# Differential heads gathered with the queries on the partitions and normed there, with rotary halves turned by DMA and narrow weights split inside one tile

## The chip, the cores and the metric

The kernel runs on one core of one Trainium2 chip. The metric is the device time of one launch, in microseconds (us); lower is better. The program is the same for every input, and all its arithmetic is done in one launch. The engines are written as the profile writes them: PE is TensorE (PEld its weight loads), DVE is VectorE, ACT is ScalarE, POOL is GpSimd, SP is the queue that issues nearly all transfers.

## The reference, cut to what matters

Three blocks run one after the other on 512 tokens of width 1024, in float32. The first has gated linear attention, a depthwise convolution of 31 taps and a spatial gate beside each other, then a feed-forward part. The second has two layers, each of feed-forward, a mixer and feed-forward. The third has a recurrent unit and blockwise attention. The change touches the two mixers most:

```
def _apply_rope(t, cos, sin):
    t1, t2 = jnp.split(t32, 2, axis=-1)
    rot = jnp.concatenate([-t2, t1], axis=-1)
    return (t32 * cos + rot * sin).astype(t.dtype)

def _hybrid_mixer(h, w_in, forget_bias, ..., subln, w_out, lambda_init):
    proj = h @ w_in
    fq, fk, fv, ff, dq, dk, dv = jnp.split(proj, IN_OFFSETS, axis=-1)
    log_f = jax.nn.log_sigmoid((ff + forget_bias).astype(jnp.float32))   # ff: 8 columns
    cum_f = jnp.cumsum(log_f.transpose(0, 2, 1), axis=-1)
    q_d = _apply_rope(to_heads_d(dq), cos, sin)
    k_d = _apply_rope(to_heads_d(dk), cos, sin)
    ...
    o_f, o_d = _causal_block_attention(q_f, k_f, v_f, cum_f, q_d, k_d, v_d, lam)
    o_d = _rmsnorm(o_d, subln) * (1.0 - lambda_init)      # over the 128 values of a head
    return jnp.concatenate([o_f, o_d], axis=-1) @ w_out

def layer_norm(x, g, b):                                  # after the convolution, over 1024 channels
    xc = xf - jnp.mean(xf, axis=-1, keepdims=True)
    ...
def gla_log_gates(a_dn, a_up, a_b):                       # a_dn: 2 x 16 columns
    z = jnp.einsum('bler,erk->blek', a_dn.reshape(bsz, L, 2, GLA_RANK), a_up) + a_b
```

There are four differential heads (two queries and two keys of 64, values of 128) and eight forgetting heads of 64 in each mixer.

## The kernel before

**Layout.** Activations lie with their channels on the partitions, so that a tile is 128 channels by 512 tokens. Products with weights keep float32's precision by splitting: every activation tile is held as a rounded part and a rest (`A.hi`, `A.lo`), every weight tile too (`WH`, `WL`), and three matmuls replace one (`products`, lines 1180 to 1182, and `K`, lines 1199 to 1201, where the tokens come out on the partitions). All other matmuls are plain float32.

**The weight pipeline.** A unit is a weight tile of 128 by 1024. SP loads it into one of five `raw` buffers, ACT rounds it into one of three `WH` (line 1574), POOL writes the rest into `WL` (line 2658), and PE uses both. ACT and POOL work two units ahead of PE in the program, SP up to seven. ACT can round a unit only when PE has used the one three before.

**The order of work.** One function, `program`, is run once for each engine; each engine's class implements the steps that it takes part in. So every engine has a fixed order, and an instruction that waits holds all behind it on its engine. Semaphores are set from events by name.

**The mixer (`second`).** With the units numbered from its start: `ff` (the forget gate; its 8 columns are padded to 128) and `dqk 0` together, the means for the norm (`roots`, line 1236), `dqk 4`, the row of norm factors (`row`, line 1266), then `diff_in` of both, `forget`, and four `K` units of `dv`, the values. `forget` is a chain of small operations on DVE and ACT that ends in running sums (`CUM`), which 16 transfers copy to the forgetting heads' queries and keys. Then come the other `dqk` tiles and `fv`. `rope(L, n)` turns tile `n` of `DQ`: PE multiplies by a constant matrix `rot` (line 1476), DVE multiplies the result by the sines, POOL multiplies the tile by the cosines in place and adds.

**Attention (`attend`).** A job is a head and a block of 128 queries: `scores` (PE, line 1486, then the mask, line 1489), a softmax over DVE and ACT, `turn` (PE transposes, line 1499, ACT copies), `gather` (PE, line 1513). Jobs are staggered: a block is turned two or three steps after its scores, and gathered later still. In each step a generator gives PE half a unit of projections (12 matmuls) to do beside, and one step of `diff_norm`. For a differential head the gather holds the values and streams the turned weights:

```
m = e.matmul(bo[a:z, qt * 128:qt * 128 + 128], at.value(h, kt, c), at.T.of(name)[:, kt * 128:kt * 128 + 128], start=kt == 0, stop=kt == qt)
```

so its output has the head's 128 values on the partitions. ACT copies it to `OD`; `diff_norm` then squares it (ACT), sums over the partitions by four matmuls against the constant `mean` (PE, line 1236), takes the root (ACT) and the reciprocal (DVE), spreads the factors over all partitions by four matmuls (PE, line 1266), copies that row (ACT) and multiplies twice (DVE).

**The convolution's norm.** PE forms the mean over all channels in one bank by eight matmuls, one for each tile of `CA` (line 1459).

## Time and profile before

| | |
|---|---|
| median of 3 runs | 3498.76 us (3498.42 to 3500.62) |
| profiled execution, its own time | 3496.82 us |
| span from its first to its last instruction | 3494.8 us |
| PE busy | 3428.0 us, 98% of the span |
| POOL busy | 1465.1 us, 42% |
| ACT busy | 1252.4 us, 36% |
| DVE busy | 1230.5 us, 35% |
| granted TensorE clock, mean of the span | 0.991 of full speed |
| read from HBM | 336.02 MB, 97 GB/s |

The table is read by shares: one engine is busy nearly all the time, the other three under half of it. A matmul is pipelined, so what it costs PE is read from the start of one to the start of the next, not from its duration. A float32 matmul that is not split shows as two records.

### The profile page before, as it was taken

What the parts mean: (1) busy time and instruction counts of PE and PEld (TensorE: products, weight loads), DVE (VectorE), ACT (ScalarE), POOL (GpSimd) and SP (SyncE); (2) the same over time, 40 slices, a digit from 0 to 9 for tenths busy, and PEclk for the clock granted to TensorE, in tenths of its full rate; (3) what the DMA queues carried; (4) which work ended last, traced back from release to release, by engine and by line L of the source; (5) the groups of instructions that cost most, each with busy time, mean ns of one, the idle gap of its engine ahead of it and who ended that gap; (6) DMA issues with size and microseconds to landing.
All of it is one profiled execution on the core that took longest, in us unless ns stands there. A gap on an engine that the chain in (4) does not pass through costs nothing.

```text
span 3494.8 us, 38815 instructions
## 1 busy us (share of the span) xinstructions
PE 3428.0 (98%) x15932; PEld 2744.4 (79%) x15932; DVE 1230.5 (35%) x2137; ACT 1252.4 (36%) x1942; POOL 1465.1 (42%) x668
## 2 busy tenths in 40 slices
PE   8999999999999999999999999999999999999998
PEld 5767787887888887887777888888887778888776
DVE  3266764523221144212653111211114652111644
ACT  4534323523222332223454222322233543222544
POOL 4323444554444444445323444444435224444332
PEclk9999999999999999999999999999999999999999
DMA  7211233442333323333113333333332023333211
GB/s 273 64 55 61 97 97 127 144 145 73 129 127 123 97 96 140 130 98 103 52 34 103 97 95 94 96 98 97 93 96 94 28 76 97 97 94 100 73 61 55
DMA packets 99291, 341.15 MB, mean 98 GB/s; under 512 B 11371, under 2 KB 11755, under 8 KB 98956
## 3 DMA queue, kind: packets, MB, share of 16 engines
q1 hardware_dynamic: 98352, 336.97, 29.8%
q8 instruction: 126, 2.06, 0.2%
q10 hardware_dynamic: 764, 1.72, 0.1%
q14 instruction: 49, 0.40, 0.0%
HBM read 336.02 MB, written 2.10 MB: 97 GB/s over the span
## 4 chain that ended last, share of the span: by engine, by line
PE 92%; DVE 2%; ACT 2%; DMA 1%; issue 1%; POOL 1%; SPq 0%; ACTq 0%; DVEq 0%
PE ps L1180 26%; PE ps L1182 25%; PE ps L1181 25%; PE ps L1199 2%; PE ps L1201 2%; PE ps L1200 2%; PE ps L1486 2%; PE ps L1513 1%; PE ps L1499 1%; DMA t<-in_w_f1i 1%; POOL t L2658 1%; PE ps L1397 0%; PE ps L1266 0%; PE ps L1411 0%; DMA t<-in_w_ada 0%
## 5 line engine op out<-in xcount | busy, mean ns | idle before, releaser
L2658 POOL TENSOR_TENSOR t<-t,t 128x1024 fp32r<-128x1024 f32 (+2 forms) x588 | 1360.9, 2316 | 1932.3 <-ACT t L1574 1931.0
L1180 PE MATMUL ps<-t,t 128*128 128x512 f32 (+1 forms) x4048 | 1608.9, 397 | 17.7 <-POOL t L2658 8.0
L1182 PE MATMUL ps<-t,t 128*128 128x512 f32 (+1 forms) x4048 | 1584.5, 391 | 0.0
L1181 PE MATMUL ps<-t,t 128*128 128x512 f32 (+1 forms) x4048 | 1578.9, 390 | 0.0
L1180 PEld LDWEIGHTS ps<-t,t 128*128 128x128 f32 x4048 | 763.7, 189 | 196.5 <-issue 27.7
L1182 PEld LDWEIGHTS ps<-t,t 128*128 128x128 f32 x4048 | 762.8, 188 | 167.9
L1181 PEld LDWEIGHTS ps<-t,t 128*128 128x128 f32 x4048 | 764.2, 189 | 158.0 <-issue 1.4
L1574 ACT CAST t<-t 128x1024 fp32r<-128x1024 f32 (+2 forms) x588 | 584.2, 995 | 576.1 <-PE ps L1182 414.8
L2451 DVE TENSOR_TENSOR t<-t,ps 128x512 f32<-128x512 f32 x110 | 75.7, 688 | 528.8 <-PE ps L1182 513.7
L1643 ACT CAST t<-t 128x512 fp32r<-128x512 f32 x158 | 97.0, 621 | 393.2 <-DVE t L2451 355.7
L1834 ACT ACTIVATE t<-t 128x512 f32<-128x512 f32 x88 | 55.6, 632 | 316.8 <-DVE t L2444 316.7
L2042 DVE TENSOR_TENSOR t<-t,t 128x512 fp32r<-128x512 f32 x138 | 119.6, 871 | 119.9 <-ACT t L1643 119.9
L2280 DVE SCALAR_TENSOR_TENSOR ps<-t,t,ps 128x392 f32<-128x392 f32 (+14 forms) x232 | 159.0, 686 | 6.2
L2412 DVE TENSOR_TENSOR t<-ps,t 128x512 f32<-128x512 f32 x32 | 22.1, 692 | 381.5 <-PE ps L1182 381.5
L2444 DVE TENSOR_TENSOR t<-ps,t 128x512 f32<-128x512 f32 x88 | 60.7, 690 | 251.0 <-PE ps L1182 225.1
L1199 PE MATMUL ps<-t,t 128*128 128x512 f32 x336 | 136.9, 407 | 8.6 <-DVE t L2188 3.9
L1871 ACT ACTIVATE t<-ps,t 128x128 f32<-128x128 f32 (+3 forms) x160 | 86.4, 544 | 151.9 <-PE ps L1499 66.3
L1201 PE MATMUL ps<-t,t 128*128 128x512 f32 x336 | 132.6, 395 | 0.0
L1200 PE MATMUL ps<-t,t 128*128 128x512 f32 x336 | 132.6, 395 | 0.0
L2507 DVE TENSOR_REDUCE t<-ps 128x1 f32<-128x128 f32 (+3 forms) x160 | 77.6, 485 | 73.3 <-PE ps L1489 72.2
L1816 ACT ACTIVATE t<-t,t 128x512 fp32r<-128x512 f32 x48 | 34.8, 724 | 157.2 <-DVE t L2414 107.5
L2094 DVE SCALAR_TENSOR_TENSOR t<-t,t,t 128x1024 f32<-128x1024 f32 x49 | 74.2, 1514 | 31.2 <-DMA t<-in_w_ada 31.1
(291 smaller groups left out, 2220.6 us busy)
## 6 DMA issues: line engine op xcount, KB each, us to landing
t<-in_w_f1i SPq DMA_DIRECT2D x88, 512.0 KB, 3.8
t<-in_w_f2i SPq DMA_DIRECT2D x88, 512.0 KB, 3.7
t<-in_w_ada SPq DMA_DIRECT2D x72, 512.0 KB, 4.6
t<-in_w_ffi SPq DMA_DIRECT2D x44, 512.0 KB, 3.9
t<-in_w_f1o SPq DMA_DIRECT2D x32, 512.0 KB, 3.5
t<-in_w_f2o SPq DMA_DIRECT2D x32, 512.0 KB, 3.5
t<-in_w_gate SPq DMA_DIRECT2D x24, 512.0 KB, 4.4
t<-in_w_out SPq DMA_DIRECT2D x48, 256.0 KB, 2.7
```

The lines of the kernel that those rows point to most:

```text
L1180: e.matmul(out, wh[:, at], X.hi[c][:, 0:N], start=c == first, stop=False)
L1181: e.matmul(out, wh[:, at], X.lo[c][:, 0:N], start=False, stop=False)
L1182: m = e.matmul(out, wl[:, at], X.hi[c][:, 0:N], start=False, stop=c == final)
L1199: e.matmul(out, X.hi[c][:, at], wh[:, w], start=c == 0, stop=False)
L1200: e.matmul(out, X.hi[c][:, at], wl[:, w], start=False, stop=False)
L1201: m = e.matmul(out, X.lo[c][:, at], wh[:, w], start=False, stop=c == 7)
L1574: e.copy(k.WH[:, n % NHL, 0:w], k.raw[:, j % NRAW, 0:w]).then_inc(*k.rounded.inc(('rounded', j)))
L1643: e.copy(A.hi[t], src).then_inc(*k.act.inc(('hi', A.tag, t)))
L1871: e.activation(p[:, 0:n], self.bank('s', *key)[:, 0:n], ACT.Exp, scale=at.root(h, qt, c) if h[0] == 'm' else 0.125, bias=st[:, 1:2], accum ...
L2042: e.tensor_tensor(A.lo[t], src, f(A.hi[t]), ALU.subtract).then_inc(*k.dve.inc(('lo', A.tag, t), *events))
L2280: e.scalar_tensor_tensor((c3 if j == 30 else a3)[:, :, lo:hi], h3[:, :, lo + w - 15:hi + w - 15], param(k, 'conv_w', w * 8 + i), a3[:, :, ...
L2658: e.tensor_tensor(k.WL[:, n % NHL, 0:w], k.raw[:, j % NRAW, 0:w], f(k.WH[:, n % NHL, 0:w]), ALU.subtract).then_inc(*k.rest.inc(('rest', j) ...
```

## The change

It has six parts.

1. **Rotary by DMA.** The matmul with `rot` goes. SP copies the two halves of each group of 64 partitions crosswise into a buffer by four transfers of 32 partitions; the sign is in the table of sines. DVE multiplies that buffer by the sines in place; two buffers take turns. There are 8 tiles in each of 2 layers.
2. **Narrow weights.** For `a`, `ff0` and `ff1` the rest of the weights (at most 32 columns) is written beside the rounded part in the same `WH` tile, so a unit needs two matmuls for each of its 8 blocks in place of three (`thin`). The two partial results come out on other partitions: for `a` the next matmul adds them (its contraction grows from 33 to 65 rows), for `ff` DVE does, with two more operations in `forget`.
3. **The mean of the convolution.** POOL adds the eight tiles into `R[0]` by seven additions, spread over the `sv` units; one matmul follows.
4. **Gather and norm of the differential heads.** The gather holds the turned weights and streams the values, so the queries lie on the partitions. ACT copies the bank to a buffer, squares it in four pieces with a sum over each row, and takes the root; DVE inverts and scales; PE transposes four blocks; ACT copies them to `OD` with the gain as a scale.
5. **Running sums.** Two transfers with a repeated source replace 16, issued behind the units of `fv` in place of before those of `dv`.
6. **Waits.** The copy of a differential head's output and the mean's copy on DVE no longer wait for the running sums and for a buffer.

```diff
+    sign = np.where(i % 64 < 32, -1.0, 1.0).astype(np.float32)[:, None]
+    cs = np.stack([np.cos(emb), sign * np.sin(emb)], axis=1).astype(np.float32)
...
+THIN = ('a', 'ff0', 'ff1')
...
+                    if n or kp:
+                        on.conv_sum(4 * n + kp)
...
+    on.cum_loads(L)
...
+            for j in range(3):
...
-    def forget(self, L, R, last):
+    def cum_loads(self, L):
         k, e = (self.k, self.e)
         self.wait_ge('forgot', L)
-        for h in range(8):
-            e.dma_start(k.QF[72:80, h, :], k.CUM[0:8, 0, :]).then_inc(*load(k, 'cum').inc(by=16))
-            e.dma_start(k.KF[64:72, h, :], k.CUM[0:8, 1, :]).then_inc(*load(k, 'cum').inc(*([('load', 'cum', L)] if h == 7 else []), by=16))
+        q, kk = (k.CUM[0:8, i:i + 1, :].broadcast_to([8, 8, S]) for i in range(2))
+        e.dma_start(k.QF[72:80, :, :], q).then_inc(*load(k, 'cum').inc(by=16))
+        e.dma_start(k.KF[64:72, :, :], kk).then_inc(*load(k, 'cum').inc(('load', 'cum', L), by=16))
+    def rope(self, L, n):
+        k, e = (self.k, self.e)
+        m = self.take(rope_ring(k, L), 'turn', L, n)
+        self.wait_ge('diff in', L, n)
+        turned = load(k, f'turned {n}')
+        for p in (0, 64):
+            e.dma_start(m[p:p + 32, :], k.DQ[p + 32:p + 64, n, :]).then_inc(*turned.inc(by=16))
+            e.dma_start(m[p + 32:p + 64, :], k.DQ[p:p + 32, n, :]).then_inc(*turned.inc(*([('turned half', L, n)] if p else []), by=16))
...
+    def thin(self, out, i, h, X, ks, c0, N, first, final):
+        k, e = (self.k, self.e)
+        wh = k.WH[:, h % NHL]
+        self.wait_ge('rest', i)
+        for c in ks:
+            at = slice(128 * (c - c0), 128 * (c - c0) + 128)
+            self.wait_ge('lo', X.tag, c)
+            e.matmul(out, wh[:, at], X.hi[c][:, 0:N], start=c == first, stop=False)
+            m = e.matmul(out, wh[:, at], X.lo[c][:, 0:N], start=False, stop=c == final)
...
-            for j in range(KT):
-                self.wait_ge('tap', j, 30)
-                m = e.matmul(b, const(k, 'mean'), k.CA[:, j, :], start=j == 0, stop=j == KT - 1)
-            m.then_inc(*k.filled.inc(('filled', ('mu',))))
+            self.wait_ge('conv sum', KT - 1)
+            e.matmul(b, const(k, 'mean'), k.R[0], start=True, stop=True).then_inc(*k.filled.inc(('filled', ('mu',))))
...
-    def rope(self, L, n):
-        k, e = (self.k, self.e)
-        b = self.take(k.banks, 'rot', L, n)
-        self.wait_ge('diff in', L, n)
-        e.matmul(b, const(k, 'rot'), k.DQ[:, n, :], start=True, stop=True).then_inc(*k.filled.inc(('filled', ('rot', L, n))))
...
-                m = e.matmul(bo[a:z, qt * 128:qt * 128 + 128], at.value(h, kt, c), at.T.of(name)[:, kt * 128:kt * 128 + 128], start=kt == 0, stop=kt == qt)
+                turned, values = (at.T.of(name)[:, kt * 128:kt * 128 + 128], at.value(h, kt, c))
+                held, moved = (turned, values) if h[0] == 'd' else (values, turned)
+                m = e.matmul(bo[a:z, qt * 128:qt * 128 + 128], held, moved, start=kt == 0, stop=kt == qt)
...
-        sq = diff_sum(at, i)
-        if j == 1:
-            self.roots(sq, 2, 8.0)
+        k, e, tag = (self.k, self.e, ('hn', at.tag, i))
         if j == 2:
-            self.row(sq)
+            b, m = (self.take(k.banks, 'turned out', at.tag, i), at.N.of(tag))
+            self.wait_ge('od scaled', at.tag, i)
+            for t in range(4):
+                x = e.transpose(b[:, t * 128:t * 128 + 128], m[:, t * 128:t * 128 + 128], const(k, 'ident'))
+            x.then_inc(*k.filled.inc(('filled', ('turned out', at.tag, i)), ('free', tag)))
...
+            m = self.take(at.N, 'hn', at.tag, i)
             self.wait_ge('filled', key)
-            self.wait_ge('load', 'cum', at.tag)
-            e.copy(k.OD[:, i, :], self.bank(*key)).then_inc(*k.act.inc(('od', at.tag, i), ('free', key)))
+            e.copy(m, self.bank(*key)).then_inc(*k.act.inc(('od', at.tag, i), ('free', key)))
...
-            m = self.take(at.N, 'hn', at.tag, i)
+            c = self.take(k.cols, 'cols', tag)[:, 0:4]
             self.wait_ge('od', at.tag, i)
-            e.activation(m, k.OD[:, i, :], ACT.Square).then_inc(*k.act.inc(('ssq', ('hn', at.tag, i), 0)))
-        if j == 1:
-            self.roots(diff_sum(at, i), 2, 8.0)
+            self.wait_ge('load', 'cum', at.tag)
+            for t in range(4):
+                w = slice(t * 128, t * 128 + 128)
+                e.activation(k.OD[:, i, w], at.N.of(tag)[:, w], ACT.Square, accum_out=c[:, t:t + 1]).then_inc(*k.act.inc())
+            self.settle()
+            e.activation(c, c, ACT.Sqrt, scale=1.0 / 128, bias=unit(k, 2)).then_inc(*k.act.inc(('root', tag)))
         if j == 2:
-            self.row(diff_sum(at, i))
+            self.wait_ge('filled', ('turned out', at.tag, i))
+            self.wait_ge('load', 'cum', at.tag)
+            e.activation(k.OD[:, i, :], self.bank('turned out', at.tag, i), ACT.Copy, scale=k.sm[:, 69:70]).then_inc(*k.act.inc(('diff normed', at.tag, i), ('free', ('turned out', at.tag, i))))
...
-    return ring(k, 'turn ' + L, k.tmp[2:3], [('forgot', L)])
+    return ring(k, 'turn ' + L, [k.R[2], k.SQ], [('filled', ('d', 'f1_' + L, 7))])
...
-        e.tensor_tensor(x, self.bank('ff', L)[0:8, :], R.acc[0:8, :], ALU.mult).then_inc(*k.dve.inc(('forget scaled', L), ('free', ('ff', L))))
+        e.tensor_tensor(x, self.bank('ff', L)[0:8, :], R.acc[0:8, :], ALU.mult).then_inc(*k.dve.inc())
+        e.tensor_tensor(y, self.bank('ff', L)[32:40, :], R.acc[32:40, :], ALU.mult).then_inc(*k.dve.inc(('free', ('ff', L))))
+        self.settle()
+        e.tensor_tensor(x, x, y, ALU.add).then_inc(*k.dve.inc(('forget scaled', L)))
...
-        m = self.take(rope_ring(k, L), 'turn', L, n)
+        m = rope_ring(k, L).of(('turn', L, n))
         self.wait_ge('load', 'cs', L)
-        self.wait_ge('filled', ('rot', L, n))
-        e.tensor_tensor(m, self.bank('rot', L, n), k.CS[:, 1, :], ALU.mult).then_inc(*k.dve.inc(('rope sine', L, n), ('free', ('rot', L, n))))
+        self.wait_ge('turned half', L, n)
+        e.tensor_tensor(m, m, k.CS[:, 1, :], ALU.mult).then_inc(*k.dve.inc(('rope sine', L, n)))
...
-        if j == 3:
-            self.wait_ge('row', tag)
-            e.scalar_tensor_tensor(x, x, param(k, 'subln_' + at.tag), diff_sum(at, i).acc, ALU.mult, ALU.mult).then_inc(*k.dve.inc(('free', tag)))
+            c = k.cols.of(('cols', tag))[:, 0:4]
+            self.wait_ge('root', tag)
+            e.reciprocal(c, c).then_inc(*k.dve.inc())
             self.settle()
-            e.tensor_scalar(x, x, at.scale, None, ALU.mult).then_inc(*k.dve.inc(('diff normed', at.tag, i)))
+            e.tensor_tensor(halves(at.N.of(tag)), halves(at.N.of(tag)), c.rearrange('p (a n) -> p a n', n=1).broadcast_to([128, 4, 128]), ALU.mult).then_inc(*k.dve.inc(('od scaled', at.tag, i), ('free', ('cols', tag))))
...
+                if src[1] in THIN:
+                    raw, wh = (ap.rearrange('p (c m) -> p c m', m=128) for ap in (k.raw[:, j % NRAW, :], k.WH[:, n % NHL, :]))
+                    e.tensor_tensor(wh[:, :, 32:64], raw[:, :, 0:32], f(wh)[:, :, 0:32], ALU.subtract).then_inc(*k.rest.inc(('rest', j), ('read', j)))
+                    continue
...
+    def conv_sum(self, i):
+        k, e = (self.k, self.e)
+        if i == 1:
+            self.wait_ge('normed', 'cx', 7)
+            self.wait_ge('tap', 0, 30)
+        else:
+            self.wait_ge('conv sum', i - 1)
+        self.wait_ge('tap', i, 30)
+        e.tensor_tensor(k.R[0], k.CA[:, 0, :] if i == 1 else k.R[0], k.CA[:, i, :], ALU.add).then_inc(*k.pool.inc(('conv sum', i)))
...
```

Three places show how instructions moved. The first is DVE in the mixer of layer 0, from the scaling of the first two tiles of `DQ` (`diff_in`, t_120) through `forget` to the first sines (t_129). Before:

```order
L2484 TENSOR_TENSOR t_120<-ps,t_71 128x512 [waits s_filled,s_act]
L2484 TENSOR_TENSOR t_120<-ps,t_71 128x512 [waits s_filled]
L2468 MEMSET t_130 8x512
L2471 TENSOR_TENSOR t_62<-ps,t_71 8x512
L2473 SCALAR_TENSOR_TENSOR t_63<-t_62,t_64 8x512 [waits s_act]
L2475 SCALAR_TENSOR_TENSOR t_65<-t_130,t_63 8x512 [waits s_dve]
L2477 TENSOR_SCALAR t_131<-t_65 8x512 [waits s_dve]
L2478 TENSOR_SCALAR t_131<-t_65 8x512
L2491 TENSOR_TENSOR t_64<-ps,t_129 128x512 [waits s_filled,s_load16,s_dve]
```

The same place in the changed kernel (its line numbers are its own):

```order
L2505 TENSOR_TENSOR t_120<-ps,t_71 128x512 [waits s_filled,s_act]
L2505 TENSOR_TENSOR t_120<-ps,t_71 128x512 [waits s_filled]
L2486 MEMSET t_130 8x512
L2489 TENSOR_TENSOR t_62<-ps,t_71 8x512
L2490 TENSOR_TENSOR t_63<-ps,t_71 8x512
L2492 TENSOR_TENSOR t_62<-t_62,t_63 8x512 [waits s_dve]
L2494 SCALAR_TENSOR_TENSOR t_63<-t_62,t_64 8x512 [waits s_act]
L2496 SCALAR_TENSOR_TENSOR t_65<-t_130,t_63 8x512 [waits s_dve]
L2498 TENSOR_SCALAR t_131<-t_65 8x512 [waits s_dve]
L2499 TENSOR_SCALAR t_131<-t_65 8x512
L2512 TENSOR_TENSOR t_72<-t_72,t_129 128x512 [waits s_load19,s_load16]
```

Two operations stand between the first scaling and the point at which ACT may start its part of `forget` (the wait for s_act), and the sine waits for transfers in place of PE. The second place is SP's queue in the same stretch. Before, behind the loads of `dqk`:

```order
L1053 DMA t_53<-in_w_dv 128x1024
L1053 DMA t_53<-in_w_dqk 128x1024 x2
L1104 DMA t_117<-t_131 8x512
L1105 DMA t_118<-t_131 8x512
L1104 DMA t_117<-t_131 8x512
```

And in the changed kernel (t_72 and t_93 are the two buffers of the turned halves):

```order
L1052 DMA t_53<-in_w_dv 128x1024
L1052 DMA t_53<-in_w_dqk 128x1024 x2
L1052 DMA t_53<-in_w_fv 128x1024 x2
L1113 DMA t_72<-t_120 32x512
L1114 DMA t_72<-t_120 32x512
L1113 DMA t_72<-t_120 32x512
L1114 DMA t_72<-t_120 32x512
L1052 DMA t_53<-in_w_fv 128x1024
L1113 DMA t_93<-t_120 32x512
```

The 16 small transfers ahead of `fv` are gone, and groups of four stand between the loads of weights. The third place is PE in attention, at the second matmul group of the first differential head's norm. Before (a group like it, L1236 x4, stands one step ahead):

```order
L1182 MATMUL ps<-t_50,t_55 128x512
L1266 MATMUL ps<-t_56,t_69 128x128 x4
L1486 MATMUL ps<-t_120 128x512 x2
L1489 MATMUL ps<-t_61 128x128 x2
L1513 MATMUL ps<-t_62,t_121 128x128 x3
L1499 MATMUL ps<-t_56,t_127 128x128
```

And in the changed kernel, where nothing stands one step ahead:

```order
L1191 MATMUL ps<-t_50,t_55 128x512
L1539 MATMUL ps<-t_56,t_65 128x128 x4
L1499 MATMUL ps<-t_120 128x512 x2
L1502 MATMUL ps<-t_61 128x128 x2
L1528 MATMUL ps<-t_121,t_62 128x128 x3
L1512 MATMUL ps<-t_56,t_127 128x128
```

Four transposes stand where the four matmuls of the row stood, and the gather (L1513, now L1528) has its two operands exchanged.

## Rows read from the trace of the kernel before

**Rows 1.** The page: PE's busy time, and the chain by engine.

```profile
PE 3428.0 (98%) x15932; PEld 2744.4 (79%) x15932; DVE 1230.5 (35%) x2137; ACT 1252.4 (36%) x1942; POOL 1465.1 (42%) x668
PE 92%; DVE 2%; ACT 2%; DMA 1%; issue 1%; POOL 1%; SPq 0%; ACTq 0%; DVEq 0%
```

**Rows 2.** Timeline of PE, products in a feed-forward part, first and last of 15.

```profile
999.71 0.39 PE L1180 MATMUL ps<-t,t 128*128 128x512 f32 x1
...
1002.88 0.39 PE L1182 MATMUL ps<-t,t 128*128 128x512 f32 x1
```

**Rows 3.** Timeline of PE, products of unit `a` for the context.

```profile
52.99 0.28 PE L1180 MATMUL ps<-t,t 128*128 128x256 f32 x1
53.11 0.28 PE L1181 MATMUL ps<-t,t 128*128 128x256 f32 x1
```

**Rows 4.** Timeline of PE, around `rot` in the value units and in attention.

```profile
1625.60 1.02 PE L1476 MATMUL ps<-t,t 128*128 128x512 f32 x2
...
1626.69 0.40 PE L1200 MATMUL ps<-t,t 128*128 128x512 f32 x1
...
1678.91 1.02 PE L1476 MATMUL ps<-t,t 128*128 128x512 f32 x2
1679.86 1.13 PE L1486 MATMUL ps<-t 64*128 64x512 f32 x4
```

**Rows 5.** Timeline of PE, the convolution's mean.

```profile
559.63 7.03 PE L1459 MATMUL ps<-t,t 128*128 128x512 f32 x16
```

**Rows 6.** Timeline of POOL, a weight rest before that mean.

```profile
553.81 2.41 POOL L2658 TENSOR_TENSOR t<-t,t 128x1024 fp32r<-128x1024 f32 x1 [3.09 <-ACT t L1574]
```

**Rows 7.** Timeline of PE, a head's norm, and four transposes.

```profile
1694.20 0.60 PE L1499 MATMUL ps<-t,t 128*128 128x128 f32 x4
...
1712.74 0.95 PE L1236 MATMUL ps<-t,t 128*128 128x2 f32 x8
1713.62 0.92 PE L1486 MATMUL ps<-t 64*128 64x384 f32 x4
...
1718.26 1.05 PE L1266 MATMUL ps<-t,t 128*128 128x128 f32 x8
1719.25 1.13 PE L1486 MATMUL ps<-t 64*128 64x512 f32 x4
```

**Rows 8.** The chain in order of time, 1588 to 1660 us.

```profile
1609.89 0.55 DVE t L2471
...
1615.84 0.95 ACT t L1574
1616.86 3.12 POOL t L2658
```

**Rows 9.** Timeline of PE, the same stretch.

```profile
1618.17 1.02 PE L1476 MATMUL ps<-t,t 128*128 128x512 f32 x2
...
1620.03 0.50 PE L1199 MATMUL ps<-t,t 128*128 128x512 f32 x1 [0.83 <-POOL t L2658]
```

**Rows 10.** Timeline of PE, two waits elsewhere.

```profile
265.67 0.50 PE L1199 MATMUL ps<-t,t 128*128 128x512 f32 x1 [3.90 <-DVE t L2188]
802.94 0.79 PE L1180 MATMUL ps<-t,t 128*128 128x512 f32 x1 [3.20 <-DVE t L2042]
```

**Rows 11.** Windows: length, busy time of each engine (records), granted clock, DMA.

```profile
89.00:95.00 6.00, 6.00 (x13) 4.13 (x13) 0.00 (x0) 5.13 (x8) 0.00 (x0) 0.50 0.01 3
262.00:272.00 10.00, 6.33 (x21) 5.08 (x22) 6.86 (x11) 6.68 (x9) 4.26 (x2) 0.83 0.09 20
798.00:812.00 14.00, 10.80 (x36) 8.32 (x35) 1.45 (x2) 3.13 (x4) 8.25 (x4) 0.76 0.35 110
1660.00:1780.00 120.00, 120.00 (x648) 91.75 (x647) 71.48 (x211) 59.00 (x142) 40.83 (x22) 1.00 0.14 45
```

**Rows 12.** Line 1104: the queue's time for one transfer of running sums.

```profile
L1104 SPq DMA_DIRECT2D t<-t x16: 624/624/729, 1622.8 to 2636.0; - x16
```

**Rows 13.** Transfers: issues, KB each, median us to landing.

```profile
out<-t SPq DMA_DIRECT2D x8, 256.0 KB, 2.0
```

More of the change, by code:

```diff
@@ L54, in shape_constants @@
     c['causal'] = np.where(t <= s, 0.0, NEG)
-    rot = np.zeros((128, 128))
-    for b in (0, 64):
-        for j in range(32):
-            rot[b + 32 + j, b + j] = -1.0
-            rot[b + j, b + 32 + j] = 1.0
-    c['rot'] = rot
     c['hmean'] = same / 64.0
@@ L812, in norms @@
                 yield
-            for j in range(4):
+            for j in range(3):
                 on.diff_norm(at, j, i)
@@ L2706, in rope @@
         self.wait_ge('load', 'cs', L)
-        self.wait_ge('filled', ('rot', L, n))
+        self.wait_ge('turned half', L, n)
         e.tensor_tensor(x, x, k.CS[:, 0, :], ALU.mult).then_inc(*k.pool.inc())
```

43 lines of the change are left out of this document (20 added, 23 removed).

## The prediction

> **What bounds the kernel now.** I read the page first. PE is busy for 98% of the span and the chain that ended last runs 92% over PE [rows 1]. So an instruction taken from PE is worth its time unless PE then waits for another engine, and an instruction added elsewhere costs nothing unless PE comes to wait for it. The second view is PE's timeline, for prices: a matmul is worth the time from its start to the next start. Fourteen steps between products take 3.17 us [rows 2], 0.226 us each; with 256 columns it is 0.12 [rows 3]. The third view is the chain in the mixer, to find where PE is not the one that sets the pace. It shows one such place: from `forget` the chain goes over DVE and ACT, ACT's rounding of a weight tile, POOL's rest of it, and only then to PE [rows 8], which sat idle 0.83 us [rows 9]. The fourth is the granted clock, because long waits of PE were followed by half clock [rows 10, 11].
>
> **Narrow weights.** Each of the four units loses 8 of 24 matmuls. `a` for the context has 256 columns: 8 × 0.12 = 0.9 us. `a` for the tokens, `ff0` and `ff1`: 24 × 0.226 = 5.4. Sum 6.4 us. POOL's part of such a unit shrinks too. I take the whole.
>
> **Rotary.** One `rot` matmul in the value units moves the product after the next from 1625.60 + 0.226 to 1626.69: 0.86 us. In attention it is 0.95 to the next group [rows 4]. There are 16: four in the value units and four in attention of each layer. The first of each layer is worth nothing, for it lies in front of the wait above: PE could have begun the next unit at 1618.2, where `rot` stands, but the weights were there only at 1620.0 [rows 9]. So each layer gains 3 × 0.86 + 4 × 0.95 = 6.4 us, together 12.8. If that wait did not exist it would be 14.5.
>
> In place of the matmul, SP issues four transfers. Its own row for a small copy inside SBUF is 0.62 us of queue [rows 12], so 2.5 us for a tile. Their landing is not in the trace; the nearest row below is the store of 256 KB, 2.0 us [rows 13], and I take that, so a tile is turned about 4.5 us after SP reaches it. At the upper end I allow twice that, 4 us of landing, if a load of weights goes ahead of it. Who waits: POOL, which stands before its cosines with the next weights behind them. In layer 0 SP may issue the first group only when the rest of the third unit of `dv` is written: 1616.86 + 3.12 [rows 8], and 1.3 later by the term on `forget` below, so 1621.3. Turned at 1626, cosines and sum done at 1629 (two passes of 128 by 512, half a weight rest each), the weights behind them (2.4 us [rows 6]) at 1631; PE wants them two units of 24 products after it began at 1621.3, so at 1632. So the cover is about 1 us for the first tile and more for the others, and I cost it at nothing. In attention DVE waits for the transfers with a softmax behind it; it waits there for the matmul already, PE turns a block two or three steps after its scores, and a step is 5.5 us (1712.74 to 1718.26 [rows 7]), which covers a delay of 2 to 3 us.
>
> **The mean.** Sixteen records take 7.03 us [rows 5]; two remain, so 14/16, 6.0 us with the drain left out. POOL takes on seven additions of 128 by 512, half the size of its weight rests of 2.4 us, so 1.2 to 1.5 us each. It idles about 3 us before each of those rests [rows 6], and the last `sv` unit leaves it time before the mean. Nothing is added.
>
> **The head's norm.** Sums cost PE 1713.62 − 1712.74 = 0.88 us, the row 1719.25 − 1718.26 = 0.99. Four transposes take 0.60 us with the drain and one alone 0.27, so 0.35 to 0.4 [rows 7]. Net 1.47 for a head, 11.7 us for eight. The gather keeps its count and shape, 128 by 128 by 128, with operands exchanged: nothing. ACT takes four squares with sums in place of one, about 0.8 us more, and has the root's table load in the same step; DVE has one pass in place of two. The scaled block is asked for one step later, and I take no wait. The lower end of this term is nothing gained, if each head's transposes wait 1.5 us.
>
> **`forget`.** Here the change costs. Two more DVE operations, each about as long as L2471 (0.55 to 0.62 us [rows 8]) and one settled on the other, put 1.3 us in front of ACT's chain, and ACT's rounding of the next weights stands behind that. So PE begins the third `dv` unit 1.3 us later than before, counted from the row of norm factors. Two layers: +2.6 us. The fewer transfers of running sums are worth nothing: the loads of `fv` behind them came in time.
>
> **The clock.** The wait of PE at that place grows. It was 0.83 us after a `rot` of 1.02; without `rot` and with 1.3 us more it is 0.83 + 0.86 + 1.3 = 3.0 us. The waits of 3.90 and 3.20 us [rows 10] lie in stretches where the clock was 0.83 over 10 us and 0.76 over 14 [rows 11], that is 1.7 and 3.4 us lost at 1.2 in place of 2.4 GHz. A wait of 3.0 us is near the short end of those that lost it, so I take it to happen in one of the two layers at 2.5 us, and keep none (0) and both at 3.4 us (6.8) for the range.
>
> **Sum.** −6.4 − 12.8 − 6.0 − 11.7 + 2.6 + 2.5 = −31.8 us. The profiled execution took 3496.8 us with a span of 3494.8; it lies 1.9 us under the median of the runs. Its sum is 3465.0; against the median, 3498.8 − 31.8 = 3467.0 us, which I predict.
>
> **Rivals.**
>
> (a) *Turned halves come late.* If the landing is 4 us or more, POOL's next weights miss PE by 1 to 2 us at the first two tiles of each layer, 4 to 8 us in all, and one wait may take the clock with it. For it: the cover is 1 us by my own count, and SP may send a load of weights just before. Against: 64 KB are little. It gives 3471 to 3480, say 3475. Chance 0.19.
>
> (b) *The clock is kept where it was lost.* After the 33-row matmuls for `a` the window 89 to 95 us ran at half clock with PE never idle [rows 11]. The change puts matmuls of 65 rows in place of those before that window; whether the clock then holds, no row shows. Those 6 us would pass in 3, so it is worth 3 us at most; with no loss in the mixers either it is 3467 − 2.5 − 3 = 3461.5. Chance 0.12.
>
> (c) *The head's norm gains nothing*, because the transposes wait for ACT's longer block and DVE's scaling. ACT is busy 59 of 120 us in that stretch and DVE 71 [rows 11], which speaks against it. 3467 + 11.7 = 3479. Chance 0.06.
>
> (d) *Transposes take the clock down.* In 1660 to 1780 us PE ran many transposes and the granted clock was 1.00 throughout [rows 11], so four more in a block should not matter. Price if each of eight heads lost the 2.5 us above: +20 us, 3487. Chance 0.02. The Trainium skill (TensorE: Matmul & The Clock Gate, Part 4: PE-mode transpose) says that a transpose does not bring the engine to its full clock as other matmuls do. By that rule the sum is 3487, by the row 3467; the trace so far goes against the rule for transposes mixed with products.
>
> (e) *Slower than before: the queue in attention.* DVE stands before each turned half with softmax work behind it. If the transfer comes later than the two steps (11 us) by which PE runs ahead, PE idles, some 3 us, and loses the clock for 2.5. With four tiles in attention of each layer that is 8 × 5.5 = 44 us, so 3511. It decides from a landing of about 8 us on (11 less 2.5 of issue); the store in rows lands in 2. Chance 0.02.
>
> **How the numbers follow.** My forecast, with no, one or two losses of clock, covers 3464 to 3471 and has 0.59. (a) 0.19, (b) 0.12, (c) 0.06, (d) and (e) 0.02 each. The range reaches down to (b), less 2 us for the lower end of what `forget` costs, and up to the middle of (a) and near (c): 3459 to 3478 leaves out about 0.15. About 0.2% (7 us) is what a measurement of this kernel can tell from no change. Everything but (e) is faster by more than that, and I keep a little for what I have not seen: faster 0.95, same 0.03, slower 0.02.
>
> **What would show each step.** PE records: 14 fewer at the mean, none at L1476's place, 32 fewer products, four one-record transposes for each head at 0.35 to 0.4 us. PE's wait before the third `dv` unit of each layer near 3 us, released by POOL, and the clock behind it. POOL's wait before its first cosines, to see whether the turned halves come about 4.5 us after SP reaches them. No new wait of PE for DVE or ACT before the transposes. I would be wrong if small copies inside SBUF cost SP or land much later than the rows nearest to them, or if PE's waits in attention grow.

## The result, and the profile after

The changed kernel took 3480.65 us (median of four runs, 3473.08 to 3481.17) beside 3498.59 of the kernel before: ratio 0.9946, 95% interval 0.9934 to 0.9958. It is faster by 17.9 us, where 31.8 were forecast, and 2.65 us above the upper end of the range. Measured again later, beside other runs of the kernel before, the same program took 3467.8 us (3466.04 to 3473.29, ratio 0.9923, interval 0.9911 to 0.9936). The second time lies 0.8 us from the forecast of 3467.0, but, as the last sections show, with other terms than the forecast's. So there are two things to explain: terms of the sum that are not there in any profile, and one that is there in some executions and not in others.

The page of the changed kernel, its line of PE and the chain by engine, answers to [rows 1]:

```profile
PE 3391.5 (98%) x15758; PEld 2721.9 (78%) x15758; DVE 1255.3 (36%) x2135; ACT 1257.6 (36%) x1998; POOL 1472.4 (42%) x675
PE 87%; DVE 4%; ACT 2%; DMA 2%; issue 1%; POOL 1%; SPq 0%; DVEq 0%; ACTq 0%; POOLq 0%
```

PE lost 36.5 us of work and the span (3478.5 us) only 16.3. PE's share of the chain fell from 92% to 87%: what went is not idle time spread thin, it is a few places where another engine now ends last. PE's waits, in us in total, times, longest:

```profile
PE ps L1189 <- POOL t L2682: 17.0, 9, 4.3
...
PE ps L1189 <- ACT t L1883: 4.8, 4, 1.6
PE ps L1220 <- DVE t L2206: 4.3, 1, 4.3
```

The timeline of PE has them one by one. These are the largest of those that are new or longer than before (the second answers to the first of [rows 10], the fourth to [rows 9]; the two near 1700 and 1711 us come again in layer 1):

```profile
101.63 0.51 PE L1189 MATMUL ps<-t,t 128*128 128x512 f32 x1 [2.37 <-POOL t L2682]
264.59 0.80 PE L1220 MATMUL ps<-t,t 128*128 128x512 f32 x1 [4.31 <-DVE t L2206]
622.35 0.80 PE L1189 MATMUL ps<-t,t 128*128 128x512 f32 x1 [3.69 <-POOL t L2682]
1617.79 0.50 PE L1220 MATMUL ps<-t,t 128*128 128x512 f32 x1 [3.05 <-POOL t L2682]
1700.22 0.50 PE L1189 MATMUL ps<-t,t 128*128 128x512 f32 x1 [0.83 <-ACT t L1883]
1711.04 0.50 PE L1189 MATMUL ps<-t,t 128*128 128x512 f32 x1 [1.57 <-ACT t L1883]
2613.25 0.50 PE L1220 MATMUL ps<-t,t 128*128 128x512 f32 x1 [3.05 <-POOL t L2682]
3241.81 0.80 PE L1189 MATMUL ps<-t,t 128*128 128x512 f32 x1 [4.26 <-POOL t L2682]
```

To see what each place costs I cut the spans at landmarks that PE has in every kernel (the first K unit behind the gates, the norm rows, the lambda matmul) and subtracted their start times. Length in us, and in brackets what of it was lost at half clock:

| stretch | before | before again | changed | changed again |
|---|---|---|---|---|
| start to the K unit at 264 | 265.7 (10.2) | 266.6 (13.7) | 264.6 (7.3) | 264.9 (9.3) |
| to the row at 663 (the mean is in it) | 398.4 (1.7) | 396.7 (0) | 398.6 (4.6) | 393.7 (2.7) |
| from there to layer 0's norm row | 942.3 (6.8) | 938.4 (5.1) | 939.5 (5.1) | 936.1 (5.1) |
| norm row to lambda, layer 0 / 1 | 37.6 / 37.6 | 37.6 / 37.7 | 39.7 (1.7) / 39.1 | 39.7 / 39.7 (1.7) |
| lambda to the row behind attention, layer 0 / 1 | 246.6 / 246.6 | 246.6 / 246.6 | 238.1 / 238.1 | 239.7 (1.7) / 238.1 |
| from there to layer 1's norm row | 719.5 | 719.5 | 717.7 | 717.7 |
| row behind layer 1's attention to the end | 600.5 (11.9) | 600.5 (11.9) | 603.1 (13.7) | 601.8 (13.7) |

Attention comes out alike to 0.1 us once the clock is taken off. The changed kernel's mixers do not (38.0 to 39.7 us), nor does the mean's stretch: 5 us lie between two executions of one program. The profiled execution of the repeat took 3473.29 us, the slowest of its five, so the table does not show what made the median 3467.8.

### The profile page after: what moved, and what is told of

Read it like the earlier page. It is cut to its first block, busy times and chain, and to the rows that moved or that the text cites. A ratio compares the mean times of both kernels' runs of the same rounds, so it can differ in the third digit from the quotient of the medians.

```text
span 3478.5 us, 38566 instructions
## 1 busy us (share of the span) xinstructions
PE 3391.5 (98%) x15758; PEld 2721.9 (78%) x15758; DVE 1255.3 (36%) x2135; ACT 1257.6 (36%) x1998; POOL 1472.4 (42%) x675
## 4 chain that ended last, share of the span: by engine, by line
PE 87%; DVE 4%; ACT 2%; DMA 2%; issue 1%; POOL 1%; SPq 0%; DVEq 0%; ACTq 0%; POOLq 0%
PE ps L1189 25%; PE ps L1191 24%; PE ps L1190 24%; PE ps L1220 2%; PE ps L1221 2%; PE ps L1222 2%; PE ps L1499 2%; PE ps L1528 1%; DVE t L2112 1%; PE ps L1512 1%; POOL t L2682 1%; DMA t<-in_w_ada 1%; DMA t<-in_w_f1i 1%; DMA t<-t 1%; PE ps L1418 1%
## 5 line engine op out<-in xcount | busy, mean ns | idle before, releaser
L1189 PE MATMUL ps<-t,t 128*128 128x512 f32 x4016 | 1598.1, 398 | 31.7 <-POOL t L2682 17.0
L1191 PE MATMUL ps<-t,t 128*128 128x512 f32 x4016 | 1573.0, 392 | 0.0
L1190 PE MATMUL ps<-t,t 128*128 128x512 f32 x4016 | 1568.4, 391 | 0.0
L1220 PE MATMUL ps<-t,t 128*128 128x512 f32 x336 | 136.0, 405 | 14.7 <-POOL t L2682 6.7
L1221 PE MATMUL ps<-t,t 128*128 128x512 f32 x336 | 133.5, 397 | 0.0
L1222 PE MATMUL ps<-t,t 128*128 128x512 f32 x336 | 133.2, 397 | 0.0
L2528 DVE TENSOR_REDUCE t<-ps 128x1 f32<-128x128 f32 (+3 forms) x160 | 77.5, 484 | 67.0 <-PE ps L1502 66.0
L2112 DVE SCALAR_TENSOR_TENSOR t<-t,t,t 128x1024 f32<-128x1024 f32 x49 | 89.2, 1821 | 33.1 <-DMA t<-in_w_ada 33.0
```

The lines of the kernel that those rows point to most:

```text
L1189: e.matmul(out, wh[:, at], X.hi[c][:, 0:N], start=c == first, stop=False)
L1190: e.matmul(out, wh[:, at], X.lo[c][:, 0:N], start=False, stop=False)
L1191: m = e.matmul(out, wl[:, at], X.hi[c][:, 0:N], start=False, stop=c == final)
L1220: e.matmul(out, X.hi[c][:, at], wh[:, w], start=c == 0, stop=False)
L1221: e.matmul(out, X.hi[c][:, at], wl[:, w], start=False, stop=False)
L1222: m = e.matmul(out, X.lo[c][:, at], wh[:, w], start=False, stop=c == 7)
```

## The experiments

The control, the changed kernel unchanged. 

> The changed kernel once more, unchanged. Expected 3480.65 us within 0.1%. Its second profile tells which waits of PE and which falls of the clock belong to the program and which to chance: the theory that the gain is lost in four fixed places expects PE to wait again 3.7 us before the first osgu gate unit (622 us), 2.4 us behind the gate logs of the context (101 us), 3.05 us before the third dv unit of each layer, and 0.8 and 1.6 us in the attention of each layer. The rival, that it is lost by chance falls of the clock, expects these waits to change from run to run.

3467.8 us. The waits at 101 us, before the third `dv` units and in attention came again to 0.1 us. Others did not: at 619.10 PE waited 0.31 us where it had been 3.69, in the last stretch 2.16 where it had been 4.26, and three waits on POOL between 1313 and 1338 us (2.5 us together) were gone, while in layer 0's mixer a wait of 1.39 us was new. So both views were partly wrong: the first places are fixed, the others differ between executions of one program. The chain in order of time shows how it comes about, first in the slower profile:

```profile
597.29 3.64 DMA t<-in_w_ada
...
600.96 3.48 DVE t L2112
...
604.45 3.92 DMA t<-in_w_ada
...
618.73 1.26 POOL t L2688
620.00 2.31 POOL t L2682
...
622.35 0.80 PE ps L1189
```

Beside the `su` units DVE takes one piece of the modulation's sum (L2112) for each unit; the pieces come through one buffer, which SP refills only when DVE has read it. That is a loop: 3.9 us of transfer, then the piece. PE passes a unit in 6.36 us, so the loop keeps up while a piece takes under 2.4. The timelines of POOL and DVE, in the slower profile:

```profile
600.95 2.40 POOL L2682 TENSOR_TENSOR t<-t,t 128x1024 fp32r<-128x1024 f32 x1
600.96 3.46 DVE L2112 SCALAR_TENSOR_TENSOR t<-t,t,t 128x1024 f32<-128x1024 f32 x1 [1.40 <-DMA t<-in_w_ada]
```

and in the faster one:

```profile
600.61 3.38 POOL L2682 TENSOR_TENSOR t<-t,t 128x1024 fp32r<-128x1024 f32 x1
600.40 1.34 DVE L2112 SCALAR_TENSOR_TENSOR t<-t,t,t 128x1024 f32<-128x1024 f32 x1 [1.17 <-DMA t<-in_w_ada]
```

Whoever starts first runs at its own pace, and the other is held: DVE needs 3.46 us in place of 1.34 when it starts 0.01 us behind POOL's weight rest, POOL 3.38 in place of 2.40 when DVE starts first. The Trainium skill (SBUF — State Buffer, section "SBUF: two separate sides") says that GpSimd and a VectorE instruction with two SBUF inputs take one port pair as an exclusive lock for a whole instruction. By that rule the trace agrees to 0.3 us: POOL's 2.40 and then DVE's 1.34 make 3.74 where DVE took 3.46, and POOL, held until DVE ended at 601.74, would take 3.53 where it took 3.38. In all eight profiles with this loop as it stands the same meeting near 600 us tells the two kinds apart: DVE starts 0.01 to 0.05 us behind POOL in the three with the long wait and ahead of it in the other five. Here 0.2 us of a transfer's landing (3.64 against 3.42 us) decided which of the two came first, and with it 5 us of the program: 3.4 of wait and 1.7 of clock.

The mean undone:

```diff
-                    if n or kp:
-                        on.conv_sum(4 * n + kp)
...
-            e.matmul(b, const(k, 'mean'), k.R[0], start=True, stop=True)
+            for j in range(KT):
+                m = e.matmul(b, const(k, 'mean'), k.CA[:, j, :], start=j == 0, stop=j == KT - 1)
```

> The changed kernel with the mean back on TensorE (16 matmuls; no additions on POOL). Theory A: of the 6.0 us that the mean gives PE, 5.2 are given back at the end of the stage, since the weights for the first gate unit behind it come no earlier; so the time rises by 0.8 us only, to about 3481.5, and PE's wait of 3.69 us there is gone. Rival B: the mean is worth its 6.0 us and the missing time is elsewhere: 3486.7 us.

3478.66 us, 10.9 more than the control beside it. The stretch took 399.3 us (2.7 lost at half clock) against 393.7 (2.7): 5.6 us, near B. Against the profile with the long wait (398.6) it is 0.7, as theory A has it, so A holds only where that wait comes. The two profiles as a whole are 5.1 us apart (3476.6 and 3471.5); that the medians are 5.8 more apart has no place that these profiles show.

Half of the sum's pieces put off:

```diff
             conv_norm()
-            ada()
+            if i % 2 == 0:
+                ada()
...
-    branch(on, 1, 'oconv', XA, k.CN, lambda j: ada() if j < 5 else None, done=mixture)
+    branch(on, 1, 'oconv', XA, k.CN, lambda j: ada() if j < 7 else None, done=mixture)
```

> The changed kernel; of the eight pieces of the modulation's sum that VectorE takes beside the eight su units (each reads one side buffer that SyncE may refill only then), four are put off to the oconv branch. Theory A: the loop over that one buffer (VectorE's piece of 2.6 to 3.5 us and 3.9 us from issue to landing, 6.8 us for a turn where PE needs 6.36 for a unit) is what makes VectorE late, and so the rest of the weights at 622 us. Then PE's wait of 3.69 us shrinks to under 1 and the time falls by 4 to 5 us, to about 3476. Rival B: POOL is late because it has the seven additions: the wait stays near 3.7 us and the time at 3480.6.

3471.19 us (3464.12 to 3474.11), no faster than the control: since the control did not have the long wait either, the runs decide nothing. In its profile the wait is gone altogether, the stretch 392.2 us.

The probe of the loop:

```diff
     def side(self, g, kt, since):
         self.wait_ge(*since)
+        if g == 2 and kt > 2:
+            self.wait_ge('mixed', kt - 3)
```

> The changed kernel; SyncE issues each further load of the side buffer of the modulation's sum only behind VectorE's product for the spatial unit two back, 1.5 to 2.5 us later than it could. A probe of the loop over that one buffer. Theory A: the loop is what makes VectorE late, its turn grows from 6.8 us to 8 or more over six turns, and PE waits at 622 us by 5 us or more in all, in every run. Rival B (POOL's seven additions): PE's wait there is what it was in the two profiles, 0.3 or 3.7 us.

3481.2 us. PE waited here too:

```profile
624.18 0.80 PE L1191 MATMUL ps<-t,t 128*128 128x512 f32 x1 [4.41 <-POOL t L2684]
```

Theory A had the wait in every run; one of the six took only 3472.76, and whether it waited is not known. In the profile the wait came, but the size was wrong: the turn grew to 6.85 us only (issues at 579.40, 586.23, 593.09, 599.93, 606.78), because the pieces, pushed to another moment, met less of POOL's rests and took 1.3 to 2.0 us. A loop of 6.85 us gives the wait without any long piece. It is the loop's turn against PE's 6.36 us that matters, and the meeting with POOL is one way to lengthen it. POOL's seven additions are the same where the wait comes and where it does not, so they do not tell the two apart; that they have no share in it is not shown. Of the eight profiles with the additions, all eight pieces and no hold (this one apart), three had the long wait.

The halves' arithmetic (DVE's sine, POOL's cosine and sum) one step behind their transfers, which `turned_half` issues:

```diff
             on.T_part(('dqk', L, n), 'dqk' + L, n, A, 0, 2)
             if turn is not None:
-                on.rope(L, turn)
+                on.turned_half(L, turn)
             yield
             on.T_part(('dqk', L, n), 'dqk' + L, n, A, 1, 2)
+            if turn is not None:
+                on.rope(L, turn)
```

> The changed kernel; in attention the four transfers of a turned half stand where they stood, but VectorE's sine and POOL's cosine and sum stand one step (half a unit) later, so the engines no longer stop in front of the transfer. Theory A: VectorE's wait of 1.6 to 1.7 us for each transfer, with its sine of 1.6 to 2.5 us beside POOL's weight rest, makes the softmax late, and with it the PSUM bank that PE's next product needs: the waits of PE of 0.83 and 1.57 us in each layer go, the time falls by about 5 us to 3476. Rival B: they come from ScalarE's longer block for the head's norm with its two table loads: the 1.57 us stay, the time falls by at most 1.7 us.

3463.17 us. Attention took 234.8 us in both layers in place of 238.1, and both waits were gone. That is 3.2 to 3.3 us for 2.40 of waiting. PE's instructions are the same and in the same order, and compared start by start the wait of 0.83 cost 1.09 us and that of 1.57 cost 1.87 (0.25 more goes ahead of them), so PE loses some 0.3 us beyond the idle time that the profile shows. So A, with a reserve for the second wait that `norm_by_sums` shows below. The timeline of DVE, the changed kernel:

```profile
1696.00 2.50 DVE L2512 TENSOR_TENSOR t<-t,t 128x512 f32<-128x512 f32 x1 [1.60 <-DMA t<-t]
1698.43 0.68 DVE L2528 TENSOR_REDUCE t<-ps 128x1 f32<-128x512 f32 x1
1699.14 0.15 DVE L2534 TENSOR_SCALAR t<-t 128x1 f32<-128x1 f32 x1
```

and POOL beside it, then ACT behind it:

```profile
1695.56 2.39 POOL L2682 TENSOR_TENSOR t<-t,t 128x1024 fp32r<-128x1024 f32 x1 [4.52 <-ACT t L1586]
...
1699.39 0.69 ACT L1883 ACTIVATE t<-ps,t 128x512 f32<-128x512 f32 x1 [3.90 <-PE ps L1512]
```

With the edit the same instruction is

```profile
1690.24 0.69 DVE L2518 TENSOR_TENSOR t<-t,t 128x512 f32<-128x512 f32 x1
```

DVE stood 1.60 us in front of the transfer and was then held by POOL's rest, 2.50 us in place of 0.69. The row maximum (L2528, L2534) came 3.4 us late, ACT's exponential behind it frees the PSUM bank that PE's next product writes, and PE waited 0.83 us at 1700.22. (The row of ACT names PE's transposes, which end at 1699.39 by the same trace; DVE's L2534 ends at 1699.29, and in layer 1 the same row names it.) In the kernel before, where the sine read PSUM, it took 0.69 us at all 16 places, each time with POOL at work beside it, and so it did in `rot_on_pe`:

```profile
1698.51 0.69 DVE L2491 TENSOR_TENSOR t<-ps,t 128x512 f32<-128x512 f32 x1 [2.06 <-PE ps L1476]
```

The rotation back on TensorE, and the head's norm by sums again (each with its own part of the change undone):

```diff
-    e.dma_start(m[p:p + 32, :], k.DQ[p + 32:p + 64, n, :])
...
+    e.matmul(b, const(k, 'rot'), k.DQ[:, n, :], start=True, stop=True)
```

> The changed kernel with the rotation by a matmul again, no transfers of turned halves. Theory A: a rot costs PE 0.82 to 0.9 us, but in attention the waits of 0.83 and 1.57 us that the transfers cause go with them: 3 x 0.82 in the value units and 4 x 0.88 - 2.4 in attention of each layer, 3.6 a layer, so the time rises by 7.2 us; the wait before the third dv unit falls from 3.05 to 2.2 us. Rival B: the transfers gave their full 12.8 us, and the time rises by that.

3474.18 us. Attention took 240.1 us, 2.0 more a layer, its two waits gone; the mixers 39.0 and, with 1.7 at half clock, 40.6, which is 0 to 1 us more for both together. In all 4 to 5 us, so nearer A than B, but under A's 7.2: the waits that A priced at 2.4 us a layer cost 3.2, and in the mixers, where other waits and the clock vary, only part of the second `rot` shows.

```diff
-            for t in range(4):
-                x = e.transpose(b[:, t * 128:t * 128 + 128], m[:, t * 128:t * 128 + 128], const(k, 'ident'))
...
+        if j == 1:
+            self.roots(sq, 2, 8.0)
+        if j == 2:
+            self.row(sq)
```

> The changed kernel with the head's norm and the gather as before (transposed gather, sums of squares and a row by TensorE). By the rows of its own profile a head's norm takes 0.53 us of TensorE (four transposes) where it took 0.88 + 0.98; so PE takes 1.33 us more for a head, 10.6 us for eight. Theory A: the term of the head's norm was about right (11.7 forecast), and the time rises by 9 to 11 us over the changed kernel's 3468 to 3481 us. Rival (c) of the prediction: the new norm gains nothing because its transposes wait; the time does not rise. In between (4 to 7 us): ScalarE's longer block has a share in the waits of 0.83 and 1.57 us of a layer's attention.

3488.76 us. Attention took 243.1 and 243.2 us with the clock taken off: 5.0 a layer, 10.1 in all, theory A. The rest of the time above the control is the long wait at 622 us, which this profile has too, and falls of the clock.

But PE's wait of 1.57 us is gone here as well, though the transfers of rotary are in place; the 0.83 us stayed. The changed kernel's ACT at that place, then ACT and PE's next product in this run:

```profile
1709.13 1.28 ACT L1883 ACT_TABLE_LOAD   x1 [0.84 <-DVE t L2534]
1710.42 0.47 ACT L1883 ACTIVATE t<-ps,t 128x256 f32<-128x256 f32 x1
...
1708.18 0.47 ACT L1884 ACTIVATE t<-ps,t 128x256 f32<-128x256 f32 x1 [3.11 <-DVE t L2528]
1709.27 0.49 PE L1189 MATMUL ps<-t,t 128*128 128x512 f32 x1
```

The new norm's root makes ACT load its table again before the next exponential, 1.28 us between DVE's late maximum and the exponential that PE waits for, and without the sums PE itself comes there 0.8 us earlier. So the second wait needs both parts of the change, the late transfer and the new norm, and goes when either is undone. Undone one at a time the two give 2.0 and 5.0 us a layer, while attention before (246.6) and after (238.1) lie 8.5 apart. Each difference is smaller by the shared wait, so their sum takes it off twice: 1.5 us a layer, 3.0 in all, are missing from it.

The two sides of `forget`:

```diff
-THIN = ('a', 'ff0', 'ff1')
+THIN = ('a',)
...
-        e.tensor_tensor(y, self.bank('ff', L)[32:40, :], R.acc[32:40, :], ALU.mult)...
-        self.settle()
-        e.tensor_tensor(x, x, y, ALU.add)...
```

> The changed kernel with the ff units at full width again (24 matmuls) and without the two added operations of VectorE in the forget chain; a stays narrow. Theory A: the added operations put 1.38 us into the chain that ends at the third dv unit, so that with them gone PE's wait there is 1.7 us in place of 3.05, against 1.8 us more of matmuls: +0.45 us a layer, +0.9 in all, less up to 1.7 for a fall of the clock that does not come. Rival B: the wait there has another cause and stays at 3.05: +3.6 us.

3475.07 us (3463.5 to 3479.1). The wait:

```profile
1616.33 0.50 PE L1220 MATMUL ps<-t,t 128*128 128x512 f32 x1 [1.68 <-POOL t L2679]
```

1.68 where A said 1.7, in the second layer 1.67, and no fall of the clock behind either; the stretch ahead of layer 1 grew by the 1.8 us of matmuls. The mixers took 37.1 and 37.3 us, where the eight profiles with the wait of 3.05 us have 39.6 on average: 2.4 us a layer back for 1.8 of matmuls. So the narrow `ff`, taken with its two operations and the clock behind them, gained nothing and cost about 0.6 us a layer.

```diff
-    on.forget(L, R, last)
     for kp in range(4):
         on.K(('dv', L), 'dv' + L, 0, A, kp, 4)
+        if kp == 0:
+            on.forget(L, R, last)
```

> The changed kernel with the forget chain written behind the first dv unit instead of ahead of it, so that ScalarE rounds the third dv unit's weights before the chain and not after it. Theory A: PE's wait of 3.05 us before the third dv unit goes in both layers, and the fourth unit's weights come in time: 6.1 us faster, and up to 1.7 us more where the clock had fallen behind the wait. Rival B: the wait only moves one unit on (POOL's rests and the turned halves stand behind the same chain): 0 to 2 us faster.

3460.95 us. The mixer's stretch fell to 34.7 us in both layers from 39.1 to 39.7: 9.3 to 10.0 us in all, more than A's 6.1 + 1.7, since a wait of 0.7 or 1.4 us two units further on (1.39 us at 1622 in the control) went too.

The narrow `a` (`THIN = ('ff0', 'ff1')`), and the kernel before again:

> The changed kernel with the two a units at full width again (24 matmuls); ff stays narrow. Theory A: behind each a unit the next weights wait for ScalarE, which has them behind the exponentials and logarithms of the gates, so that PE's wait of 2.37 us at 101 us shrinks by what the matmuls take more; the narrow a units were worth at most the 0.9 us of the context's, and the time to the first K unit behind them (264 us) stays within 1 us. Rival B: they were worth their 2.7 us, and that stretch grows by it.

3473.6 us. PE's wait behind the token's unit:

```profile
102.91 0.50 PE L1189 MATMUL ps<-t,t 128*128 128x512 f32 x1 [0.60 <-POOL t L2682]
```

2.37 − 0.60 = 1.77 us, the eight matmuls (1.81). The windows from the context's gate logs to the next landmark behind that unit, for the kernel before, the repeat of the changed kernel and this run (length, busy time by engine, and the granted clock as the third number from the end):

```profile
85.55:108.85 23.30, 23.30 (x82) 16.95 (x81) 2.53 (x4) 14.19 (x20) 7.15 (x3) 0.85 0.22 71
88.57:109.18 20.61, 18.24 (x73) 13.46 (x72) 2.53 (x4) 14.11 (x20) 7.03 (x3) 1.00 0.21 70
87.83:108.49 20.66, 20.06 (x82) 14.96 (x81) 2.54 (x4) 14.21 (x20) 7.10 (x3) 1.00 0.24 76
```

With wide or narrow `a` the stretch takes the same 20.6 us. So A for the tokens' unit. Whether the context's unit gave its 0.9 us no run can tell: it lies in a stretch that varies by more than that from one execution to the next.

> The kernel before once more, for a second profile of it. Expected: the same time within 0.1%, the same waits of PE in the mixers and in attention; what differs between its two profiles (falls of the clock behind one and the same wait, PE's waits of 0.7 to 0.8 us at 1315 to 1340 us) is chance and belongs to no edit.

3494.57 us, ratio 0.9993 (0.9982 to 1.0004). The wait of 3.90 us at 266 us was 0.72 here, behind more half clock at the start, and those at 1315 to 1340 us summed to 0.3 us, not 2.3. The waits in the mixers and in attention were the same.

All three gains together (pieces put off, arithmetic one step later, `forget` behind the first unit):

> The changed kernel with three edits together: rotary's sine and cosine one step behind their transfers, the forget chain behind the first dv unit, four pieces of the modulation's sum put off. By the stages of the single profiles: attention 234.8 us in place of 238.1, the mixers 34.7 in place of 38.0 (and no fall of the clock there), twice each, so 13.2 us less than the changed kernel, and none of the 5 us at 622: 3454 to 3456 us. Rival: the turned halves, asked for by POOL right behind the forget chain, take part of it back: 3458 to 3461 us.

3455.54 us (3452.89 to 3457.28), ratio 0.9882 (0.9866 to 0.9899): faster than both kernels, and where the stretches put it (3454 to 3456).

## Why the prediction was wrong, point by point

**The method.** Taking PE as the bound and pricing a matmul from start to start was right, and so were the sizes where PE stayed the bound. What failed is "costs nothing, for it lies beside other work": three times the cover was thinner than I had it.

**Narrow weights.** Forecast −6.4. The two `ff` units gave 3.6, 1.8 each, as forecast (seen in layer 1; layer 0's lies in a stretch that varies by more), and more than that went again in `forget` and the clock, below. The tokens' `a` gave nothing of its 1.8 (`a_wide`): behind it ACT takes the gates' exponentials and logarithms ahead of the next weights, which come when they come. For the context's `a`, 0.9, the runs do not decide. "I take the whole" was the failed step; it had no look at who ends last behind each unit.

**Rotary.** Forecast −12.8; 4 to 5 us came beside the new norm. The price of a `rot` was right: `rope_later` is 5.3 us a layer below `rot_on_pe` in attention's stretch (234.8 and 240.1), where two `rot` of 0.86 and four of 0.95 make 5.5. And with the two waits away the stretch is 11.8 us shorter than before, where these and four norms of 1.47 make 11.4. The transfer was near too: 0.59 us of queue, 2.6 us to landing where I took 2.0, and in layer 0's mixer the first tile was there at 1623.7, not 1626. The failed step is "a step is 5.5 us, which covers a delay of 2 to 3 us". DVE was delayed by 1.6 us of waiting and by 1.8 more that I had not priced: the sine used to read PSUM and now has two operands in SBUF, so POOL's rest holds it. Nor had I priced that PE's waits cost more than their length (3.2 us for 2.4). This is rival (a) in attention, not in the value units where I had put it.

**The mean.** Forecast −6.0. The stretch gives 5.6 in one pair of profiles and nothing in three of eight (398.6 to 399.9 us, where the mean on PE takes 399.3). The step "nothing is added" looked at POOL, and POOL had the time. It did not look at DVE, whose loop over one buffer takes 4.8 to 7.2 us a turn (from issue to issue of SP) beside PE's 6.36. That the mean's 7 us on PE had let the loop catch up fits the runs, for with the mean on PE no profile has the wait, but no run shows it apart.

**The head's norm.** Forecast −11.7; undone beside the transfers it measures −10.1, and with the rotation by matmul in both kernels (246.6 against 240.1 us in attention, parts 5 and 6 of the change included) −13.0. The price was right; what "I take no wait" missed is the second table load, which shares in the wait of 1.57 us. Four transposes take 0.53 us in the first two heads (1713.92 to 1714.45) and 0.44 in the next two, not 0.35 to 0.4:

```profile
1713.92 0.60 PE L1539 MATMUL ps<-t,t 128*128 128x128 f32 x4
1714.45 0.70 PE L1499 MATMUL ps<-t 64*128 64x512 f32 x2
```

No wait stands before them, so rival (c) fell, and no row shows a cost of the exchanged operands. Rival (d) fell too. The windows of the changed kernel, the mixer of layer 0 and its attention, have the clock behind the last mean:

```profile
1602.75:1642.40 39.65, 35.68 (x153) 28.80 (x152) 15.47 (x17) 15.78 (x18) 21.14 (x10) 0.96 0.34 103
1642.40:1880.51 238.11, 230.37 (x1251) 176.69 (x1252) 130.42 (x349) 119.45 (x295) 87.25 (x48) 1.00 0.23 69
```

**`forget` and the clock.** Forecast a wait of 3.0 us; it was 3.05 in both layers, of which the two operations are 3.05 − 1.68 = 1.37 us (1.3 forecast): +2.8 in all. Half clock followed one of the two in each profile of the changed kernel, at 1.7 us and not 2.5. Over eight profiles with that wait it followed 11 of 16 and took 3.0 us a program on average. Keeping the clock did not always pay. In the repeat's layer 0 it stayed, and PE was too early for the weights two units on:

```profile
1622.27 0.50 PE L1189 MATMUL ps<-t,t 128*128 128x512 f32 x1 [1.39 <-POOL t L2682]
```

That mixer took 39.7 us, as much as the one at half clock; the four others that kept the clock took 38.1 to 39.1.

**Rival (b)**, that the half clock at 89 to 95 us goes: it went, and I had given it a chance of 0.12. The stretch around it took 23.3 us in both profiles of the kernel before and 20.6 to 20.7 in nine of the twelve profiles of the changed kernel and its variants, 2.6 us less where I had 3 at most. In the other three, the first profile of the changed kernel among them, half clock came behind the wait at 101 us (1.7 us lost), and the stretch took 22.3. What kept the clock, the 65-row matmuls or something else, no run shows; narrow `a` it was not, for `a_wide` has it too.

**The sum as measured:** −3.6 for `ff`, 0 for the tokens' `a`, −2.6 for rival (b) (−1.0 in the first profile), −4.5 for rotary and −10.1 for the norm, each undone alone, −3.0 because these two take the shared wait off twice, −5.6 or about 0 for the mean, +2.8 for `forget`, +3.0 for the clock: −24 with the mean, −18 without. The runs gave −17.9 and −29.9. The first fits to 1.5 us: its profile has the long wait that takes the mean's gain. Over all nine runs of the changed kernel the median is 3473.1 us, some 23 us under the kernel before. The 6 us between −24 and −29.9 have no term and no profile, for of those five executions the slowest was the one profiled. Some places differ between profiles though no edit touched them: the POOL waits near 1315 to 1340 us (none in one profile, 2.5 us in another), and the last stretch, 251.9 us in one profile and 256.6 in another. Why the first runs drew the slow side and the later ones the fast side stays open.

So 3467.8 us against a forecast of 3467.0 is luck: rotary fell 8 us short, the narrow `a` 2 to 3 and the norm alone 1.6, and rival (b), the 3.0 us of the shared wait and 6 us without a term made up for it.

## What to carry to other kernels

Taking work from the engine that bounds gives its price only until the next engine in line ends last, so ask at each place what sets the arrival behind it, and how much later it may be. A wait on a transfer belongs one step behind its issue, and a long chain on a shared engine belongs behind the small urgent job that others wait for: moving lines alone gave some 14 us on top of the change (ratio 0.9882 to the kernel before, where the change alone had 0.9923). And two parts of a change can share one wait: each undone alone shows it as its own, so the sum of the two differences is less than what they give together. When VectorE's operand moves from PSUM to SBUF, price it again beside what GpSimd runs at that moment (0.69 us against up to 2.73 here).

## What was not expected of the hardware

An operation of DVE with two SBUF operands took 3.46 us beside one of POOL and 1.34 ahead of it; which comes first can hang on 0.2 us of a transfer, so one program has two times 5 us apart. And one and the same wait of 3.05 us lowered the clock in one layer and not in the next. Two windows of 10 us, behind the third `dv` unit of layer 0 and of layer 1:

```profile
1617.00:1627.00 10.00, 9.21 (x33) 7.44 (x34) 4.23 (x3) 1.49 (x2) 6.50 (x5) 0.83 0.56 159
2612.00:2622.00 10.00, 8.75 (x39) 7.25 (x40) 5.08 (x4) 2.00 (x3) 6.54 (x4) 1.00 0.55 158
```
